# Newton steps of the inverse roots on whole columns, and the merge of two branches in PSUM banks, in a one-core two-block forward pass

## The reference, cut to what matters

```python
def rms_norm(x, w):
    xf = x.astype(jnp.float32)
    return (xf * lax.rsqrt(jnp.mean(xf * xf, axis=-1, keepdims=True) + RMS_EPS)).astype(x.dtype) * w
...
        y_a = o @ w_o_nsa[i]
...
        y_b = c @ w_conv_out[i] + b_conv_out[i]

        ga, gb = jnp.split(jax.nn.sigmoid(zm), 2, axis=-1)
        h = h + (ga * y_a + gb * y_b) @ w_out[i]
```

## Time and profile before

| | us |
|---|---|
| median of three runs | 964.98 |
| profiled execution, its own time | 967.93 |
| span of the profiled execution | 966.1 |
| PE busy | 891.1 (92%) |
| DVE busy | 586.1 (61%) |
| ACT busy | 483.3 (50%) |
| POOL busy | 620.0 (64%) |

### The profile page before, as it was taken

How to read it: one execution, slowest core, us unless ns; L and a number is a source line. 1 busy time by engine, 2 the same in 40 slices (tenths; PEclk the granted TensorE clock), 3 DMA queues, 4 the chain that set the end, 5 groups by cost and what they waited for, 6 DMA issues and landing times.

```text
span 966.1 us, 18261 instructions
## 1 busy us (share of the span) xinstructions
PE 891.1 (92%) x7019; PEld 852.7 (88%) x7019; DVE 586.1 (61%) x1582; ACT 483.3 (50%) x920; POOL 620.0 (64%) x274
## 2 busy tenths in 40 slices
PE   7999899989998899999998995978989999999995
PEld 7999888879997799999988984857879999999995
DVE  6986567762255544443479867676666666751155
ACT  6754465534544365555535364444445454454451
POOL 3899645537885356548777794222366888878970
PEclk9999999998999999999999898889999999999998
DMA  8577432223654243445555564121245666666621
GB/s 323 178 218 216 136 110 88 89 66 109 193 179 131 73 125 110 134 129 153 175 155 155 168 204 127 49 84 47 85 131 153 197 190 192 181 187 179 200 84 44
DMA packets 38534, 138.85 MB, mean 144 GB/s; under 512 B 4272, under 2 KB 4272, under 8 KB 38448
## 3 DMA queue, kind: packets, MB, share of 16 engines
q1 hardware_dynamic: 38448, 137.69, 46.9%
HBM read 136.63 MB, written 1.05 MB: 142 GB/s over the span
## 4 chain that ended last, share of the span: by engine, by line
PE 65%; DVE 16%; issue 3%; ACT 3%; POOL 1%; DVEq 0%; ACTq 0%
PE ps L538 17%; PE ps L540 17%; PE ps L539 17%; DVE ps L1379 2%; DVE ps L1525 2%; DVE nnm L1673 1%; PE ps L733 1%; DVE root L1383 1%; PE ps L571 1%; PE ps L735 1%; PE ps L545 1%; POOL wl L499 1%; PE ps L547 1%; PE ps L546 1%; PE ps L563 1%
## 5 line engine op out<-in xcount | busy, mean ns | idle before, releaser
L499 POOL TENSOR_TENSOR wl<-raw,wh 128x1024 fp32r<-128x1024 f32 x254 | 608.5, 2417 | 297.5 <-ACT wh L970 297.5
L538 PE MATMUL ps<-uh,wh 128*128 128x256 f32 x1248 | 357.3, 286 | 5.3 <-DVE ul L1460 2.2
L539 PE MATMUL ps<-ul,wh 128*128 128x256 f32 x1248 | 352.1, 282 | 0.0
L540 PE MATMUL ps<-uh,wl 128*128 128x256 f32 x1248 | 351.8, 282 | 0.0
L970 ACT ACTIVATE wh<-raw 128x1024 fp32r<-128x1024 f32 x256 | 263.1, 1054 | 124.7 <-PE ps L540 121.5
L538 PEld LDWEIGHTS ps<-uh,wh 128*128 128x128 f32 x1248 | 238.7, 191 | 11.1 <-issue 4.1
L539 PEld LDWEIGHTS ps<-ul,wh 128*128 128x128 f32 x1248 | 238.8, 191 | 0.0
L540 PEld LDWEIGHTS ps<-uh,wl 128*128 128x128 f32 x1248 | 238.5, 191 | 0.0
L1618 DVE TENSOR_TENSOR h<-ps,h 128x256 f32<-128x256 f32 x32 | 13.6, 425 | 118.4 <-PE ps L540 118.3
L538 PE MATMUL ps<-ffh,wh 128*128 128x256 f32 x176 | 49.1, 279 | 0.0
L539 PE MATMUL ps<-ffl,wh 128*128 128x256 f32 x176 | 49.1, 279 | 0.0
(11 more groups left out here) (355 smaller groups left out, 1835.0 us busy)
## 6 DMA issues: line engine op xcount, KB each, us to landing
raw<-slabs SPq DMA_DIRECT2D x256, 512.0 KB, 3.7
h<-x_fm SPq DMA_DIRECT2D x4, 256.0 KB, 5.3
out_fm<-outb SPq DMA_DIRECT2D x4, 256.0 KB, 2.2
cst<-shape_consts SPq DMA_DIRECT2D x1, 768.0 KB, 7.8
vec<-vectors SPq DMA_DIRECT2D x1, 303.5 KB, 4.0
pin<-p_fm SPq DMA_DIRECT2D x1, 256.0 KB, 4.1
```

Source lines behind the costliest of these rows:

```text
L499: nc.gpsimd.tensor_tensor(wl[:, s % PART_RING, :], raw[:, s % RAW_RING, :], wh[:, s % PART_RING, :].bitcast(f32), ALU.subtract).then_inc(s ...
L538: nc.tensor.matmul(res, w_h, a_h, start=first, stop=False)
L539: nc.tensor.matmul(res, w_h, a_l, start=False, stop=False)
L540: ins = nc.tensor.matmul(res, w_l, a_h, start=False, stop=last)
```

## The change

The estimate of a Newton root is kept twice, in SBUF (`dst`) and in PSUM (`nw_r`, eight more columns of the same bank as the other small tiles), and every step works on all columns of the root at once with tensor operands in place of pointers: y = r * dst, e = y * msq into a new SBUF tile `step`, and (e + 1.5) * r written once to SBUF and once to PSUM. Each of y, e and the PSUM copy of r is linked. The guess is written twice too. The products around n_mix take whole columns.

In the merge, the gated product of tile n goes to the right half of PSUM bank 4 or 5 (by the parity of n), and the sum to its left half; ACT and `merge_low` read the sum from there. `merge_low(n - 1)` moves from behind the sum of n to between the product and the sum of n. The wait for the sum before (`merged`) gives way to one for `merge_lo`, n - 1.

```diff
-        nw_m, nw_y, nw_s = PS_M[:, 8:16], PS_M[:, 16:24], PS_M[:, 24:32]
+        nw_m, nw_y, nw_s, nw_r = PS_M[:, 8:16], PS_M[:, 16:24], PS_M[:, 24:32], PS_M[:, 32:40]
...
+        def merge_gated(n):
+
+            return PS_S[n % 2][:, T:2 * T]
+
+        def merge_sum(n):
+            return PS_S[n % 2][:, 0:T]
...
-                nc.scalar.activation(mh[:, n, :], mt[:, n, :], ACT.Copy).then_inc(sem("merge_hi"), 1)
+                nc.scalar.activation(mh[:, n, :], merge_sum(n), ACT.Copy).then_inc(sem("merge_hi"), 1)
...
             def newton(dst, width, last=None):
 
+                r, y, e, m = nw_r[:, 0:width], nw_y[:, 0:width], step[:, 0:width], msq[:, 0:width]
                 for i in range(NEWTON):
-                    for b in range(width):
-                        ins = ts(one(nw_y, b), one(dst, b), one(dst, b), one(msq, b), ALU.mult, ALU.mult)
-                    link(ins)
-                    to = dst if last is None or i + 1 < NEWTON else last
-                    for b in range(width):
-                        ins = ts(one(to, b), one(nw_y, b), 1.5, one(dst, b), ALU.add, ALU.mult)
+                    link(tt(y, r, dst, ALU.mult))
+                    link(tt(e, y, m, ALU.mult))
                     if i + 1 < NEWTON:
-                        link(ins)
-                return ins
+                        stt(dst, e, 1.5, r, ALU.add, ALU.mult)
+                        link(stt(r, e, 1.5, r, ALU.add, ALU.mult))
+                return stt(dst if last is None else last, e, 1.5, r, ALU.add, ALU.mult)
...
-                    for b in range(TB):
-                        ins = ts(one(nw_s, b), one(sums, b), one(root1, b), one(root1, b), ALU.mult, ALU.mult)
-                    link(ins)
-                    sums = nw_s[:, 0:TB]
-                ts(nw_m[:, 0:width], sums, 1.0 / n.width, EPS, ALU.mult, ALU.add)
+                    sums_ = nw_s[:, 0:TB]
+                    link(tt(sums_, sums, root1[:], ALU.mult))
+                    link(tt(sums_, sums_, root1[:], ALU.mult))
+                    sums = sums_
+                m = nw_m[:, 0:width]
+                ts(m, sums, 1.0 / n.width, EPS, ALU.mult, ALU.add)
                 link(ts(msq[:, 0:width], sums, -0.5 / n.width, -0.5 * EPS, ALU.mult, ALU.add))
-                link(ts(dst[:, 0:width].bitcast(i32), nw_m[:, 0:width].bitcast(i32), -0.5, 1597463007.0, ALU.mult, ALU.add))
+                ts(dst.bitcast(i32), m.bitcast(i32), -0.5, 1597463007.0, ALU.mult, ALU.add)
+                link(ts(nw_r[:, 0:width].bitcast(i32), m.bitcast(i32), -0.5, 1597463007.0, ALU.mult, ALU.add))
                 if n is n_mix:
-                    link(newton(dst, width, nw_s))
-                    for b in range(TB):
-                        ins = ts(one(late_tok, b), one(nw_s, b), one(root1, b), None, ALU.mult)
+                    link(newton(dst, width, nw_s[:, 0:TB]))
+                    ins = tt(late_tok[:], nw_s[:, 0:TB], root1[:], ALU.mult)
...
             def merge_low(n):
                 dve.wait_ge(sem("merge_hi"), n + 1)
-                tt(ml[:, n, :], mt[:, n, :], mh[:, n, :].bitcast(f32), ALU.subtract).then_inc(sem("merge_lo"), 1)
+                tt(ml[:, n, :], merge_sum(n), mh[:, n, :].bitcast(f32), ALU.subtract).then_inc(sem("merge_lo"), 1)
...
-                wait(dve, "merged", n)
-                tt(yat[:], o[:, 0:T], gm[:, n, :], ALU.mult).then_inc(sem("dve_evac"), 1)
-                dve.wait_ge(sem("dve_evac"), freed[jobs[f"ya{n}"].out][1])
-                tt(mt[:, n, :], mt[:, n, :], yat[:], ALU.add).then_inc(sem("merged"), 1)
+                wait(dve, "merge_lo", n - 1)
+                tt(merge_gated(n), o[:, 0:T], gm[:, n, :], ALU.mult).then_inc(sem("dve_evac"), 1)
                 if n:
                     merge_low(n - 1)
+                dve.wait_ge(sem("dve_evac"), freed[jobs[f"ya{n}"].out][1])
+                tt(merge_sum(n), merge_gated(n), mt[:, n, :], ALU.add).then_inc(sem("merged"), 1)
```

More of the change, by code:

```diff
@@ L246, in build @@
         sqsum = sb("sqsum", [P, 2, T])
-        msq, root = sb("msq", [P, 2 * TB]), sb("root", [P, 2 * TB])
+        msq, root, step = sb("msq", [P, 2 * TB]), sb("root", [P, 2 * TB]), sb("step", [P, 2 * TB])
         late = sb("late", [P, T])
@@ L1371, in low_part @@
                 tt(n.lo(k), n.sqb(k), n.hi(k).bitcast(f32), ALU.subtract).then_inc(sem("norm_lo"), 1)
-            one = lambda t, b: t[:, b:b + 1]
             def newton(dst, width, last=None):
+                r, y, e, m = nw_r[:, 0:width], nw_y[:, 0:width], step[:, 0:width], msq[:, 0:width]
                 for i in range(NEWTON):
-                    for b in range(width):
-                        ins = ts(one(nw_y, b), one(dst, b), one(dst, b), one(msq, b), ALU.mult, ALU.mult)
-                    link(ins)
-                    to = dst if last is None or i + 1 < NEWTON else last
-                    for b in range(width):
-                        ins = ts(one(to, b), one(nw_y, b), 1.5, one(dst, b), ALU.add, ALU.mult)
+                    link(tt(y, r, dst, ALU.mult))
+                    link(tt(e, y, m, ALU.mult))
                     if i + 1 < NEWTON:
-                        link(ins)
-                return ins
+                        stt(dst, e, 1.5, r, ALU.add, ALU.mult)
+                        link(stt(r, e, 1.5, r, ALU.add, ALU.mult))
+                return stt(dst if last is None else last, e, 1.5, r, ALU.add, ALU.mult)
             def inverse_root(n):
@@ L1393, in inverse_root @@
                 sums, width = PS_M[:, n.col:n.col + n.groups * TB], n.groups * TB
-                dst = root1 if n is n_fin1 else root
+                dst = (root1 if n is n_fin1 else root)[:, 0:width]
                 if n is n_mix:
                     dve.wait_ge(sem("norm_root"), n_fin1.i + 1)
-                    for b in range(TB):
-                        ins = ts(one(nw_s, b), one(sums, b), one(root1, b), one(root1, b), ALU.mult, ALU.mult)
-                    link(ins)
-                    sums = nw_s[:, 0:TB]
-                ts(nw_m[:, 0:width], sums, 1.0 / n.width, EPS, ALU.mult, ALU.add)
+                    sums_ = nw_s[:, 0:TB]
[4 more added lines that the diff above has]
+                ts(m, sums, 1.0 / n.width, EPS, ALU.mult, ALU.add)
                 link(ts(msq[:, 0:width], sums, -0.5 / n.width, -0.5 * EPS, ALU.mult, ALU.add))
-                link(ts(dst[:, 0:width].bitcast(i32), nw_m[:, 0:width].bitcast(i32), -0.5, 1597463007.0, ALU.mult, ALU.add))
+                ts(dst.bitcast(i32), m.bitcast(i32), -0.5, 1597463007.0, ALU.mult, ALU.add)
+                link(ts(nw_r[:, 0:width].bitcast(i32), m.bitcast(i32), -0.5, 1597463007.0, ALU.mult, ALU.add))
                 if n is n_mix:
-                    link(newton(dst, width, nw_s))
-                    for b in range(TB):
-                        ins = ts(one(late_tok, b), one(nw_s, b), one(root1, b), None, ALU.mult)
+                    link(newton(dst, width, nw_s[:, 0:TB]))
+                    ins = tt(late_tok[:], nw_s[:, 0:TB], root1[:], ALU.mult)
                 else:
```

## The result

The changed kernel takes 948.79 us (median of four runs, 947.84 to 951.94) where the kernel before, beside it on the same chip, takes 965.03 (four runs, 963.9 to 965.2). The ratio is 0.9832, with a 95% interval of 0.9806 to 0.9857: 1.4 to 1.9% faster, 16.2 us between the medians. The profiled execution took 947.84 us (span 946.0, mean clock 0.975), 20.1 us less span than that of before.

A forecast was written before the change was run, and what follows sets the result against it. TensorE, busy 92% of the span, sets the pace, so its waits can be won: Newton 11.0 + merge 5.8 = 16.8 us off the profiled 967.93, and 2.95 lower for the median, gives 948.2 us, range 940 to 957.

The forecast's parts named there:

- n_mix: Roots n_fin1 and n_mix: 1.1 us less waiting and 1.55 us from a clock that stays up, 2.7 us together.
- the merge: Merge before wo: PSUM operands make each VectorE operation 0.42 us; 4.5 us idle and 1.27 us clock loss go, 5.8 us.
- n_ple: Root at n_ple, where TensorE waits 1.97 us: 0.6 us gained, with the clock drop staying.
- p: Time of one linked Newton step on VectorE, taken as 0.20 us (unlinked 0.08), upper bound 0.31; a root takes 10p + 0.20.
- The whole Newton part: All Newton roots together: 3.7 + 3.1 + 2.7 + 1.5 = 11.0 us gained.
- The SSM groups: Six SSM groups: the narrow root's whole 0.61 us comes through to TensorE in each, 3.7 us.
- The wide root: Four-column root of the last SSM group: 2.45 us less waiting and 0.65 from the clock in its spread, 3.1 us.
- The clock doesn't recover: Rival: remaining waits at n_mix or in wo0 still drop TensorE's clock; 3.5 us less gain, 951.7 us; chance 0.11.
- The count decides: Rival: each tiny Newton instruction costs 0.22 us, linked or not, so narrow roots gain nothing; 956.4 us; chance 0.08.
- The merge is still held: Rival: a tile of mt stays in SBUF and POOL still holds the merge's sum; gain 11.0, 954.0 us; chance 0.03.
- The slower rival: Rival: each linked Newton step crossing between PSUM and SBUF costs 0.50 us; 985.7 us; chance 0.03.
- the unknown of 2 to 4 us: SBUF operations outside the change meet POOL at other moments; one or two hits are 2 to 4 us, either sign.

The follow-up runs named there:

- three more links: The changed kernel with three more waits in each Newton root and the same instructions: 954.18 us, ratio 0.9852 to the kernel before.
- the moved maxima: The changed kernel with the NSA row maxima and the gated embedding's product also moved to PSUM: 945.23 us, ratio 0.9752 to the kernel before.

## Why the prediction was right, point by point

**The time.** Forecast 948.2 us, range 940 to 957; measured 948.79. The sum, 16.8, and the difference of the medians, 16.2, agree; the terms did so less well than the sum, and a part of the agreement is luck: in the last group of runs the same two kernels lie 20.0 us apart (968.7 and 948.65), n_mix gave less than its term, and n_ple and the merge more.

**The Newton steps.** p = 0.20 and 0.08 were taken from rows of like operands; the root came out at 2.15 us for 2.20. The whole Newton part, forecast at 11.0 us, gave 10.8 by its own timed runs. Root by root:
- The SSM groups gave 3.6 for 3.7, and their spreads follow each other in 11.43 us instead of 12.05. The choice between the weight loads' wait (0.76, so the whole 0.61 comes through) and the matmuls' own idle time (0.47) went the right way: both waits are gone in all six groups.
- The wide root gave 2.47 of idle time for 2.45 and 0.9 in its spread, which now takes 1.16 us for 2.07, where 0.65 was forecast.
- The waits for the root fell by 6.9 us (11.7 to 4.8); counted by matmuls, the prediction's terms give 2.8 + 2.45 + 0.6 + 0.6 + 0.3 = 6.75.
- **n_mix** was mis-sized: 2.0 for 2.7. The wait and what stood behind it gave 1.4 (1.1 was said), the clock 0.6 and not 1.55. The step that failed takes matmul time lost at the lower level as time on the path; TensorE waits for ksT 40 us later, and most of it was spare. That the first idle stretch alone makes the drop was too simple as well: two profiles have the stretch and no drop.
- **n_ple**: "the clock drop stays" was wrong. With 1.32 us of idle time in place of 1.97 the clock stayed up, in every profile with the new steps there, 1.70 with the three more links included; with 1.97 or 1.98 it fell in every one. From that spread to TensorE's next wait it now takes 25.5 us instead of 26.7, and the whole stretch gave 2.0 for 1.2.

**The merge.** All three operations take 0.41 to 0.43 us under POOL, the idle time is gone, the clock stays up: as forecast. Its size was set too low. Of the 8.0 us that the merge gave in this pair of profiles (9.6 against the kernel before profiled again, 8.7 against the Newton part alone) 4.5 are the idle time, as said; the rest, sized at 1.27, is the clock and the distance of the matmuls, which the runs don't separate. The clock's share was read from one profile, in which 712 to 719 us, with the last wait in it, hold 41 matmuls at a mean clock of 0.76. The kernel before once more has 27 at 0.52 in the seven microseconds there:

```profile
710.00:717.00 7.00, 5.88 (x27) 5.88 (x28) 1.98 (x3) 1.76 (x3) 3.15 (x2) 0.52 0.35 85
```

In timed runs the merge gave 5.4 or 8.1 on top of the Newton part, and 3.1 alone. Why it is less alone is open; the 1.0 us that the SSM groups lose there is a part of it. The bounds for the moved low part (0 to 2 us) were paid at 0.

**The rivals.** "The clock doesn't recover" did not come about in any of the three stages that it names: the granted clock is 1.00 behind n_mix, in wo0 and in the spread of the wide root. "The count decides" fell by the three links (at the 0.22 a step that it names, the wide root would go from 4.65 to 2.81, which is 1.8 less and not 2.2, and the case would be 956.8). "The merge is still held" fell by the single lines. The slower rival had a wrong mechanism, as a step that crosses between PSUM and SBUF costs no more than another. The danger was one that the prediction did not price: the same steps between SBUF tiles alone are 30 us slower than before. The rows named it for the merge, but it was not carried over to the Newton steps, where the upper bound of p, 0.31, was read from undisturbed rows. The PSUM copy of the estimate is what the gain hangs on.

**What was not forecast.** Three stretches changed without a cause that is shown. NSA gained 5.3 us in the profiles; over the profiles without the moved maxima it takes 150.6 to 156.0, and the kernel before took 152.7 the second time, so most of this is scatter, the unknown of 2 to 4 us that the range held. The start lost 1.2; it takes 111.3 us in another profile of the changed kernel, so that is scatter too. The stretch from the wide root to n_mix lost 1.5: 267.7 to 269.6 with the old steps in four profiles, 269.2 to 269.8 with the new ones. It follows the distance of the matmuls, on average 0.1167 to 0.1170 us in the profiles with 267.7 to 268.4 and 0.1177 or 0.1178 in those with 269.2 to 269.8. As the merge alone, with the Newton steps of before, shows both in its two profiles, those steps alone don't set it; what does stays open. Scatter of this kind also explains why the profiles differ by 20.1 us and the medians by 16.2: the profiled execution of before was 2.9 above its median, that of after 0.95 below.

## What to carry to other kernels

Where GpSimd runs long instructions, a small VectorE operation between SBUF tiles on a dependent chain is priced not by its own 0.16 us but by what is left of GpSimd's instruction, up to 2.4 us, and a chain of them makes one step per such instruction; one operand in PSUM takes the hold away, and even an additional instruction to keep a copy there pays. Price a chain of tiny operations by its waits (0.20 us linked, 0.07 not), not by its count. And a clock drop costs only what no later wait would have taken anyway, so look for the next wait before counting it.

## What the runs showed that was not expected

- An operation on 128x2 is held as long as one on 128x256: up to 2358 ns for one of 161, and 4869 for a scaling of 170 (line 1677, in the changed kernel profiled again and with three more links).
- The clock behaves differently after like waits: at n_mix, idle stretches of 1.13 and 0.98 us with a short spread between were followed by a clock of 0.57 in one kernel and 1.00 in another. At n_ple it always fell after 1.97 and never after 1.70 or less.
- The distance of matmuls that follow each other without idle time is not the same in two executions of one kernel: 1587 and 1572 of them in 185 us of the feed-forward of the kernel before. That is 1.7 us in this stretch alone, as much as some of the terms of the prediction.
